# Strassen's seven products for two of the four output column blocks of a feed-forward layer

## Chip, cores and metric

The kernel runs on one core of a Trainium2 chip. The metric is the device time of one launch in microseconds, the median over several runs. The core has TensorE (PE, matrix products; its weight loads are PEld), VectorE (DVE), ScalarE (ACT), GpSimd (POOL) and SyncE (SP, which issues most DMAs). Each engine works through its own queue in order; semaphores tie the queues together.

## What is computed

A decoder trunk of two layers on a sequence of 256 tokens with 2048 features, all in float32. Layer 0 mixes by retention and pooling, layer 1 by sliding-window attention. Both end in the same kind of feed-forward block, and that block is what the change is about:

```python
def conv_glu_ffn(x, w_in, conv_w, conv_b, w_out):      # x (1, 256, 2048)
    h = x @ w_in                                       # 2048 x 11264
    hp = jnp.pad(h, ((0, 0), (2, 0), (0, 0)))
    hc = conv_b + hp[:, 0:S] * conv_w[0]
    for kk in range(1, 3):
        hc = hc + hp[:, kk:kk + S] * conv_w[kk]
    gate, val = jnp.split(hc, 2, axis=-1)
    return (jax.nn.gelu(gate, approximate=False) * val) @ w_out   # 5632 x 2048
...
x = layer_norm(ALPHA * x + ffn, ln_gain, ln_bias)
```

## The kernel before

**Weights.** All weight matrices are streamed once from HBM in groups of 128 partitions x 4 k-tiles x 512 columns (1 MB). A group s is loaded by SP into `raw[:, s % 6]` (the ring has `RING = 6` places), ScalarE rounds it to fp32r into `w_hi` (`high(s)`, L475), and VectorE writes the remainder `raw - w_hi` in place as `w_lo` (`low(s)`, L752). TensorE then makes a product of float32 quality out of three fp32r products: activations high x weights high, high x weights low, low x weights high. When it has finished a group it raises `used`; SP waits for `used` of the group six places back before it loads again. ScalarE issues `high` four groups ahead of the group that it is keeping step with (`HI_LEAD = 4`), VectorE `low` three ahead (`LO_LEAD = 3`).

**The feed-forward block.** The 5632 hidden features are cut into FC = 11 chunks of 512. For each chunk c the kernel makes

- the gate projection (`hidden`, 4 groups): the weights stand still, the 256 tokens move, once as high and low together (512 columns, L1270) and once as high alone (256 columns, L1280). The result lies in four PSUM banks, transposed;
- the value projection (`hidden`, 4 groups), into the other four banks;
- for each of two pairs of banks of either kind: ScalarE copies the low half out of PSUM (`halves`, L539), VectorE adds it (`pair_sum`, L782) and makes the causal convolution of three taps (`convolve`, L1004 and L1007); ScalarE takes the GELU of the gate, VectorE multiplies value and gate (L1027) into `gated`, and the two split that into high and low in `gT` (L622, L1032);
- the output product (`output`, 4 groups, one for each column block n of 512): for each of the two token halves of 128, twelve matmuls of 512 columns (`plain_tile`, L1297 to L1299: 4 k-tiles x 3 products). VectorE adds each block to the residual `xres` (`add_chunk`, L786, 128 x 1024).

TensorE's order is gate(0), value(0), and then nine turns of a hardware loop with gate(c+1), output(c), value(c+1) on banks 0 to 3, 4 to 7, 4 to 7; the last chunk is written out behind the loop, with output(9) and output(10) at its end, and the layer norm follows. The convolution parameters of the running chunk are copied into `cur` (L1022) since a loop can't name them.

`lnp` holds the layer norm's gain and bias (2 x 2048 words in each partition, each filled by a broadcasting load of 1 MB).

Of the kernel before, what the change touches and what calls it, by code (L numbers as in the profile page):

```python
# [52 lines left out]
ARENA = 14080  # L53
# [17 lines left out]
FFN_GROUPS = 3 * KG * FC  # L71
# [4 lines left out]
S_FFN = [S_FFN0, S_FFN1]  # L76

# [36 lines left out]
TURNS = FC - 2  # L114
LOOP_OWN = 12


class Count:


    def __init__(self):
        self.n, self.turn, self.per, self.start = 0, None, 0, 0

    def now(self):
        return self.n if self.turn is None else self.n + self.turn * self.per

    def enter(self, turn, per):
        self.turn, self.per, self.start = turn, per, self.n

    def leave(self, turns):  # L130
        assert self.n - self.start == self.per, (self.n - self.start, self.per)
        self.n, self.turn = self.start + self.per * turns, None


def build_trunk(nc, x, ln_gain, ln_bias, even_w_in, pool_w, pool_scale, even_w_out, attn_w_qkv, attn_b_qkv,
# [10 lines left out]
    with ExitStack() as ctx:  # L146
# [25 lines left out]
        ln_eps = sb("ln_eps", [P, 1])  # L172
        arena = sb("arena", [P, ARENA])

# [52 lines left out]
        conv_v = take(TPC, SEQ)  # L227
        gated = take(TPC, SEQ)
        cur = sb("cur", [P, 2, 4, TPC])
# [52 lines left out]
        ffn_added = sem("ffn_added")  # L282
        akv_ready = sem("akv_ready")
# [35 lines left out]


        @block.sync
        def _(sp):
            def load(s, source, turn=0):

                if not isinstance(turn, int) or s >= RING:

                    sp.wait_ge(used, s - RING + 1 + turn * 12)
                sp.dma_start(raw[:, s % RING], source).then_inc(raw_landed[s % RING], 16)
# [15 lines left out]
            def hidden(l, s, c, value, turn=0):  # L344
                for kg in range(KG):
                    load(s + kg, w_ffn_in[l][:, GK * kg:GK * kg + GK, bass.ds(c * COLS + value * D_FF, COLS)],
                         turn)

            def output(l, s, c, turn=0):
                for n in range(NCH):  # L350
                    load(s + n, w_ffn_out[l][:, bass.ds(c * GK, GK), cols(n * COLS)], turn)

            def ffn(l):
                base = S_FFN[l]
                hidden(l, base, 0, 0)
                hidden(l, base + KG, 0, 1)
                hidden(l, base + 2 * KG, 1, 0)
                output(l, base + 3 * KG, 0)

                sp.wait_ge(ln_chunk, TOK * NCH * (2 * l + 1))  # L360
                load_params(2 * l + 1)
                hidden(l, base + 4 * KG, 1, 1)
                with sp.Fori(1, TURNS) as turn:
                    s = base + 2 * KG
                    hidden(l, s, turn + 1, 0, turn)
                    output(l, s + KG, turn, turn)
                    hidden(l, s + 2 * KG, turn + 1, 1, turn)

                tail = base + FFN_GROUPS - 4 * KG
                hidden(l, tail, FC - 1, 0)  # L370
                hidden(l, tail + KG, FC - 1, 1)
                output(l, tail + 2 * KG, FC - 2)
                output(l, tail + 3 * KG, FC - 1)
# [74 lines left out]
        def _(pool):  # L448
# [5 lines left out]

            pool.wait_ge(gain_ready, 4)
# [10 lines left out]
        def _(act):  # L466
            def high(s, turn=0):

                if s >= S_END:
                    return  # L470
                act.wait_ge(raw_landed[s % RING], 16 * (s // RING + 1) + turn * (16 * (12 // RING)))
                if not isinstance(turn, int) or s >= RING:

                    act.wait_ge(used, s - RING + 1 + turn * 12)
                nc.scalar.activation(w_hi[:, s % RING], raw[:, s % RING], ACT.Copy).then_inc(hi_ready, 1)  # L475
# [54 lines left out]
            def halves(n, bank, ended, turn=0):  # L530

                if n == TP_ODD + 7:
                    act.wait_ge(queries_half, 1)
                else:
                    act.wait_ge(used, ended + turn * 12)
                if not isinstance(turn, int) or n >= 2:

                    act.wait_ge(added, n - 1 + turn * 4)
                nc.scalar.activation(half[:, n % 2], ps[:, bank:bank + 2, SEQ:2 * SEQ], ACT.Copy) \  # L539
                    .then_inc(half_out, 1)  # L540
# [74 lines left out]
            def gelu(n, q, turn=0):  # L615
                act.wait_ge(conv_done, n + turn * 2)
# [3 lines left out]
            def gated_high(n, q, turn=0, to=gT):  # L620
                act.wait_ge(gated_out, n + turn * 2)
                nc.scalar.activation(to[:, 2 * q:2 * q + 2, 0:SEQ], gated[:, 2 * q:2 * q + 2], ACT.Copy) \  # L622
                    .then_inc(g_hi, 1)

            def feed_forward(l):
                base, tp, gp = S_FFN[l], TP_FFN[l], 2 * FC * l
                norm_fill(2 * l, base)
                for j in range(1, 8):
# [12 lines left out]
                    if j in (6, 7):  # L641
                        gelu(gp + j - 5, j - 6)
                with act.Fori(0, TURNS) as turn:
                    s = base + 2 * KG
                    for j in range(12):
                        high(s + j + HI_LEAD, turn)
                        if j == 0:

                            for q in range(2):
# [1147 lines left out]
```

## Time and profile before

| | |
|---|---|
| median of 3 runs | 2062.64 us (2062.59 to 2062.69) |
| span of the profiled execution, first to last instruction | 2061.1 us |
| median of the runs less that span | 1.5 us |
| PE busy | 2052.3 us (100%) |
| DVE busy | 1444.6 us (70%) |
| ACT busy | 887.1 us (43%) |
| POOL busy | 5.8 us |
| read from HBM | 386.36 MB |

The profiled execution has no time of its own besides its span; the 1.5 us is what a launch has around it if the profiled execution ran like the others. An engine's busy time counts from the start of an instruction to its end; consecutive instructions of an engine can overlap by some hundredths of a microsecond, so what one costs a queue is the distance from its start to the start of the next one.

### The profile page before, as it was taken

How to read it: one execution, taken by the hardware profiler on the slowest of the kernel's cores; microseconds unless marked ns; L12 is line 12 of the kernel's file. 1: busy time of each engine (PE TensorE's matmuls, PEld its weight loads, DVE VectorE, ACT ScalarE, POOL GpSimd, SP SyncE). 2: the span in 40 equal slices, each digit the busy share in tenths (PEclk: the TensorE clock that was granted, in tenths of full speed). 3: DMA queues.
4: the chain of work that ended last, by engine and by line, in shares of the span. 5: the costliest groups of instructions: out<-in, count | busy, mean ns of one | idle time of the engine just before them, and what ended most of it. 6: DMA issues, size and time to landing. Idle time of an engine off the chain costs nothing.

```text
span 2061.1 us, 27212 instructions
## 1 busy us (share of the span) xinstructions
PE 2052.3 (100%) x10924; PEld 1756.3 (85%) x10924; DVE 1444.6 (70%) x1641; ACT 887.1 (43%) x825; POOL 5.8 (0%) x10
## 2 busy tenths in 40 slices
PE   9999999999999999999999999999999999999998
PEld 8888888888888888888888877888888888888887
DVE  5446566767767687677697886786776768766768
ACT  5433443543443434434434555354344344444342
POOL 0000000000000000000000000000000000000000
PEclk9999999999999999999999999999999999999999
DMA  9654474655555565555555435465555555555552
GB/s 331 196 191 145 142 258 163 235 197 187 188 196 186 187 198 184 186 199 184 188 186 190 144 123 190 162 241 194 194 184 193 193 184 195 191 184 195 191 184 102
DMA packets 194766, 389.57 MB, mean 189 GB/s; under 512 B 6970, under 2 KB 9748, under 8 KB 193684
## 3 DMA queue, kind: packets, MB, share of 16 engines
q1 hardware_dynamic: 194419, 388.49, 56.6%
q8 instruction: 42, 0.69, 0.1%
q10 hardware_dynamic: 288, 0.26, 0.1%
q14 instruction: 17, 0.13, 0.0%
HBM read 386.36 MB, written 2.10 MB: 188 GB/s over the span
## 4 chain that ended last, share of the span: by engine, by line
PE 98%; DVE 1%; DMA 0%; SPq 0%; issue 0%; ACT 0%; DVEq 0%
PE ps L1270 36%; PE ps L1280 19%; PE ps L1297 13%; PE ps L1299 12%; PE ps L1298 12%; PE ps L1420 1%; PE ps L1711 1%; PE ps L1686 1%; PE ps L1694 1%; PE ps L1387 0%; PE ps L1425 0%; PE ps L1258 0%; PE ps L1537 0%; DMA xres<-x 0%; DVE xres L810 0%; PE ps L1338 0%
## 5 line engine op out<-in xcount | busy, mean ns | idle before, releaser
L475 ACT ACTIVATE w_hi<-raw 128x2048 fp32r<-128x2048 f32 x352 | 673.9, 1916 | 951.1 <-DMA raw<-ffn_w_in 523.7
L752 DVE TENSOR_TENSOR w_lo<-raw,w_hi 128x2048 fp32r<-128x2048 f32 x352 | 800.9, 2287 | 220.0 <-ACT w_hi L475 219.2
L1270 PE MATMUL ps<-T,w_hi 128*128 128x512 f32 x3264 | 765.0, 390 | 0.0
L1270 PEld LDWEIGHTS ps<-T,w_hi 128*128 128x128 f32 x3264 | 605.7, 188 | 122.9 <-issue 1.7
L1280 PEld LDWEIGHTS ps<-T,w_lo 128*128 128x128 f32 x3264 | 405.8, 192 | 10.0 <-issue 2.0
L1280 PE MATMUL ps<-T,w_lo 128*128 128x256 f32 x3264 | 410.6, 283 | 0.0
L1297 PE MATMUL ps<-w_hi,gT 128*128 128x512 f32 x704 | 274.2, 389 | 0.0
L1299 PE MATMUL ps<-w_hi,gT 128*128 128x512 f32 x704 | 273.9, 389 | 0.0
L1298 PE MATMUL ps<-w_lo,gT 128*128 128x512 f32 x704 | 273.9, 389 | 0.0
L782 DVE TENSOR_TENSOR arena<-ps,half 128x512 f32<-128x512 f32 x96 | 65.5, 688 | 183.6 <-ACT half L539 183.6
L786 DVE SCALAR_TENSOR_TENSOR xres<-ps,xres 128x1024 f32<-128x1024 f32 (+1 forms) x103 | 117.9, 1144 | 89.1 <-PE ps L1299 87.9
L1297 PE MATMUL ps<-w_hi,T 128*128 128x512 f32 (+1 forms) x448 | 177.4, 396 | 0.1
L1299 PE MATMUL ps<-w_hi,T 128*128 128x512 f32 (+1 forms) x448 | 174.0, 388 | 0.0
L1298 PE MATMUL ps<-w_lo,T 128*128 128x512 f32 (+1 forms) x448 | 173.6, 388 | 0.0
L1007 DVE SCALAR_TENSOR_TENSOR arena<-arena,cur 128x256 f32<-128x256 f32 x352 | 155.1, 482 | 6.3
L1297 PEld LDWEIGHTS ps<-w_hi,gT 128*128 128x128 f32 x704 | 132.1, 188 | 28.0 <-DVE arena L1230 0.3
L1299 PEld LDWEIGHTS ps<-w_hi,gT 128*128 128x128 f32 x704 | 132.1, 188 | 27.4
L1298 PEld LDWEIGHTS ps<-w_lo,gT 128*128 128x128 f32 x704 | 132.2, 188 | 27.4
L1297 PEld LDWEIGHTS ps<-w_hi,T 128*128 128x128 f32 x448 | 84.2, 188 | 19.9 <-DVE T L843 2.7
L1299 PEld LDWEIGHTS ps<-w_hi,T 128*128 128x128 f32 x448 | 84.1, 188 | 17.6
L1298 PEld LDWEIGHTS ps<-w_lo,T 128*128 128x128 f32 x448 | 84.3, 188 | 16.2
L1004 DVE TENSOR_SCALAR arena<-arena,cur 128x256 f32<-128x256 f32 x176 | 64.7, 410 | 3.3
(159 smaller groups left out, 802.9 us busy)
## 6 DMA issues: line engine op xcount, KB each, us to landing
raw<-ffn_w_in SPq DMA_DIRECT2D x176, 1024.0 KB, 5.0
raw<-ffn_w_out SPq DMA_DIRECT2D x88, 1024.0 KB, 5.0
raw<-even_w_in SPq DMA_DIRECT2D x38, 1024.0 KB, 5.1
raw<-attn_w_qkv SPq DMA_DIRECT2D x20, 1024.0 KB, 5.2
raw<-even_w_out SPq DMA_DIRECT2D x16, 1024.0 KB, 5.0
raw<-attn_w_out SPq DMA_DIRECT2D x16, 1024.0 KB, 5.1
arena<-ln_gain SPq DMA_DIRECT2D x4, 1024.0 KB, 6.3
arena<-ln_bias SPq DMA_DIRECT2D x4, 1024.0 KB, 8.3
```

The costliest lines, as they stand in the source:

```text
L475: nc.scalar.activation(w_hi[:, s % RING], raw[:, s % RING], ACT.Copy).then_inc(hi_ready, 1)
L752: vec.tensor_tensor(w_lo[:, s % RING], raw[:, s % RING], w_hi[:, s % RING].bitcast(F32), ALU.subtract).then_inc(lo_ready, 1)
L782: vec.tensor_tensor(to, ps[:, bank:bank + 2, 0:SEQ], half[:, n % 2], ALU.add).then_inc(added, 1)
L786: return vec.scalar_tensor_tensor(at, ps[:, bank], 1.0 / ALPHA, at, ALU.mult, ALU.add)
L1004: ins = vec.tensor_scalar(conv[:, i], h[:, i, 0:SEQ], cur[:, kind, 0, i:i + 1], cur[:, kind, 3, i:i + 1], ALU.mult, ALU.add)
L1007: ins = vec.scalar_tensor_tensor(conv[:, i], h[:, i, k:k + SEQ], cur[:, kind, k, i:i + 1], conv[:, i], ALU.mult, ALU.add)
L1270: ins = mm(ps[:, banks[j]], w_hi[:, s % RING, k, P * j:P * j + P], T[:, GK * kg + k], start=kg == 0 and k == 0, stop=kg == KG - 1 and k == ...
L1280: ins = mm(ps[:, banks[j], 0:SEQ], w_lo[:, s % RING, k, P * j:P * j + P], T[:, GK * kg + k, 0:SEQ], start=False, stop=False)
L1297: mm(ps[:, bank, 0:n], x_hi, w_hi[:, s % RING, k, c], start=start and k == 0, stop=False)
L1298: mm(ps[:, bank, 0:n], x_hi, w_lo[:, s % RING, k, c], start=False, stop=False)
L1299: ins = mm(ps[:, bank, 0:n], x_lo, w_hi[:, s % RING, k, c], start=False, stop=stop and k == GK - 1)
L1420: mm(ps[:, a], T[:, t, lo:lo + P], w_hi[:, s, k], start=False, stop=False)
```

## The change

Two chunks of hidden features, a = 2p and b = 2p + 1, are taken together (a "duo", five in each layer, `DUOS = 5`; chunk 10 is left over and goes through an ordinary output product, the tail). For column blocks 0 and 1 the product [256 tokens x 1024 hidden] x [1024 x 1024 columns] is cut into 2 x 2 blocks: token halves x the two chunks on one side, the two chunks x the two column blocks on the other. Seven products of blocks replace eight. Each needs a form of the activations (a block of `gated` or a difference of such: `X_11, X_21, D_3, X_12, X_22, D_1, D_2, D_4`) and a block or sum of blocks of the weights (`SUM_12, W_11, W_22, SUM_24, SUM_124, W_21, SUM_ALL`). Column blocks 2 and 3 keep the plain product, with the two chunks summed in PSUM before they are read (`pair_output`).

- Weights of the seven (names as indices 0 to 6 in TensorE's order): `W_11`, `W_22`, `W_21` are loaded. `SUM_24` is loaded with one block, and GpSimd then issues two DMAs, one behind the other, of two k-tiles each (512 KB), that add the fourth block from HBM onto it. `SUM_12`, `SUM_124` and `SUM_ALL` are additions on VectorE (128 x 2048 each). The first two stand in `weight_sums`, the third in `last_weight_sum`. They are put in the place of `lnp`, which is loaded only near the end of the layer.
- Order on TensorE in a duo: gate(a+2), value(a+2), the seven products (`quad`), gate(b+2), value(b+2), four groups of `pair_output`.
- The seven results go from PSUM to `xres` in nine additions of 128 x 512 (`take_product`), some with the sign -1; three of them read a bank into which two or three products were summed.
- Each group that is only a sum takes a place in `w_hi` but none in the ring of loads.
- The hardware loops are gone: the program is written out, and `cur` with it.

The core of the diff:

```diff
+            for l in range(2):                       # GpSimd
+                for p in range(DUOS):
+                    i, q = DUOS * l + p, S_FFN[l] + Q_AT[p]
+                    pool.wait_ge(*landed(q + SUM_24))
+                    pool.wait_ge(summed, 3 * i + 1)
+                    for j in range(2):
+                        t = GK * (2 * p + 1) + 2 * j
+                        pool.dma_start(raw_at(q + SUM_24)[:, 2 * j:2 * j + 2], w_ffn_out[l][:, t:t + 2, COLS:2 * COLS],
+                                       accum_op=ALU.add).then_inc(second_summed, 16)
+                        pool.wait_ge(second_summed, 32 * i + 16 * (j + 1))
...
+                if s in SUMS and SUMS[s][0] == SUM_24:          # ScalarE, high(s)
+                    act.wait_ge(second_summed, 32 * (DMA_SUMS.index(s) + 1))
+                elif s in SUMS:
+                    act.wait_ge(summed, SUMS[s][1])
+                else:
+                    act.wait_ge(*landed(s))
...
+                def weight_sums(p):                             # VectorE
+                    q, n = base + Q_AT[p], 3 * (DUOS * l + p)
+                    dve.wait_ge(*landed(q + W_11))
+                    dve.wait_ge(*landed(q + SUM_24))
+                    vec.tensor_tensor(raw_at(q + SUM_12), raw_at(q + W_11), raw_at(q + SUM_24), ALU.add) \
+                        .then_inc(summed, 1)
+                    dve.wait_ge(*landed(q + W_22))
+                    dve.wait_ge(summed, n + 1)
+                    vec.tensor_tensor(raw_at(q + SUM_124), raw_at(q + SUM_12), raw_at(q + W_22), ALU.add) \
+                        .then_inc(summed, 1)
...
+                    s = base + V_AT[a]
+                    for j in range(KG):
+                        if j < 2:
+                            gate_pair(a, j, x)
+                        if j == 1:
+                            weight_sums(p)
+                        low(s + j + LO_LEAD)
+                    s = base + Q_AT[p]
+                    low(s + LO_LEAD)
+                    dve.wait_ge(used, s + 1)
+                    last_weight_sum(p)
+                    take_product(p, 0, x, 1, 1, -1.0)
+                    low(s + 1 + LO_LEAD)
+                    dve.wait_ge(used, s + 2)
+                    take_product(p, 1, x + 1, 0, 0, 1.0)
+                    low(s + 2 + LO_LEAD)
+                    dve.wait_ge(used, s + 3)
+                    take_product(p, 2, x, 0, 1, -1.0)
+                    low(s + 3 + LO_LEAD)
+                    dve.wait_ge(used, s + 4)
+                    take_product(p, 3, x + 3, 1, 1, -1.0, 1)
+                    low(s + 4 + LO_LEAD)
+                    dve.wait_ge(used, s + 5)
+                    take_product(p, 4, x + 1, 0, 1, -1.0, 3)
+                    take_product(p, 5, x + 1, 1, 0, 1.0)
+                    take_product(p, 6, x + 1, 1, 1, -1.0, 4)
+                    dve.wait_ge(used, s + 6)
+                    take_product(p, 7, x + 2, 0, 0, 1.0, 2)
+                    dve.wait_ge(used, s + 7)
+                    take_product(p, 8, x + 3, 1, 0, 1.0, 6)
...
+                s = base + C_AT[DUOS - 1]                       # VectorE, end of a layer
+                for j in range(KG):
+                    if j == 2:
+                        dve.wait_ge(used, s + 2)
+                        add_chunk(2, 0, ffn_added)
+                    low(s + j + LO_LEAD)
+                    if j < 2:
+                        value_pair(c, j, 4)
+                    else:
+                        gated_low(j - 2)
...
+            def form_product(s, f, bank, start, stop=True, more=False):     # TensorE
+                for k in range(GK):
+                    x_hi, x_lo = form_at(f)[:, k, 0], form_at(f)[:, k, 1]
+                    w, last = w_hi[:, s % RING, k], stop and k == GK - 1
+                    mm(ps[:, bank], x_hi, w, start=start and k == 0, stop=False, skip_group_check=more)
+                    mm(ps[:, bank], x_hi, lo_at(s)[:, k], start=False, stop=False, skip_group_check=more)
+                    ins = mm(ps[:, bank], x_lo, w, start=False, stop=last, skip_group_check=more)
+                return ins
...
+                def quad(p, x):
+                    s, r = base + Q_AT[p], READS * (DUOS * l + p)
+                    pe.wait_ge(form_ready, FORMS * (DUOS * l + p + 1))
+                    pe.wait_ge(*evicted(2 * p + 2, 0)[1])
+                    ready(s)
+                    form_product(s + SUM_12, D_1, x, True).then_inc(used, 1)
+                    ready(s + W_11)
+                    form_product(s + W_11, X_11, x + 1, True).then_inc(used, 1)
+                    ready(s + W_22)
+                    pe.wait_ge(quad_read, r + 1)
+                    form_product(s + W_22, D_4, x, False, more=True).then_inc(used, 1)
+                    ready(s + SUM_24)
+                    form_product(s + SUM_24, D_3, x + 3, True).then_inc(used, 1)
...
+                    out_block(l, q + W_11, a, 0)                # SP, order of loads in a duo
+                    out_block(l, q + W_22, b, 1)
+                    out_block(l, q + SUM_24, a, 1)
+                    out_block(l, q + W_21, b, 0)
```

`quad_read` counts the nine `take_product` of a duo; the third product waits for the first of them, the fifth for the second, the seventh for the fourth, and gate(b+2) for the seventh and the ninth. SP's load of a group waits for `used` of the load six places back in the ring of loads, which for `SUM_24` is the first group of value(a+2), and for `W_21` the second.

## Rows read from the trace of the kernel before

**Rows 1.** The page: busy time by engine, clock in 40 slices, the chain.
```profile
PE 2052.3 (100%) x10924; PEld 1756.3 (85%) x10924; DVE 1444.6 (70%) x1641; ACT 887.1 (43%) x825; POOL 5.8 (0%) x10
...
PEclk9999999999999999999999999999999999999999
...
PE 98%; DVE 1%; DMA 0%; SPq 0%; issue 0%; ACT 0%; DVEq 0%
```

**Rows 2.** Timeline of PE: start us, us, engine, line, names, shapes, count.
```profile
564.18 3.79 PE L1270 MATMUL ps<-T,w_hi 128*128 128x512 f32 x16
567.81 4.00 PE L1280 MATMUL ps<-T,w_lo 128*128 128x256 f32 x32
571.64 7.44 PE L1270 MATMUL ps<-T,w_hi 128*128 128x512 f32 x32
...
608.64 0.39 PE L1297 MATMUL ps<-w_hi,gT 128*128 128x512 f32 x1
608.86 0.39 PE L1298 MATMUL ps<-w_lo,gT 128*128 128x512 f32 x1
...
630.40 3.79 PE L1270 MATMUL ps<-T,w_hi 128*128 128x512 f32 x16
```

**Rows 3.** Groups of DVE over two turns of the loop, 602 to 734.2.
```profile
L752 DVE TENSOR_TENSOR w_lo<-raw,w_hi 128x2048 fp32r<-128x2048 f32 x25 | 57.0, 2287 | 16.4 <-ACT w_hi L475 16.2
L1007 DVE SCALAR_TENSOR_TENSOR arena<-arena,cur 128x256 f32<-128x256 f32 x32 | 14.1, 482 | 0.6
L786 DVE SCALAR_TENSOR_TENSOR xres<-ps,xres 128x1024 f32<-128x1024 f32 x8 | 9.8, 1223 | 6.0 <-PE ps L1299 5.9
```

**Rows 4.** Busy times in stretches: engines, clock, DMA share, GB/s.
```profile
602.00:734.20 132.20, 132.20 (x705) 114.54 (x704) 93.62 (x101) 54.12 (x40) 0.00 (x0) 1.00 0.58 190
10.00:15.00 5.00, 4.59 (x28) 4.11 (x29) 3.82 (x7) 3.17 (x6) 0.00 (x0) 1.00 1.05 401
2055.00:2061.00 6.00, 0.67 (x2) 0.00 (x0) 3.35 (x5) 0.69 (x1) 0.00 (x0) 0.93 0.66 253
```

**Rows 5.** Timeline of DVE in one turn of the loop.
```profile
588.72 0.69 DVE L782 TENSOR_TENSOR arena<-ps,half 128x512 f32<-128x512 f32 x1 [3.75 <-ACT half L539]
...
592.76 2.28 DVE L752 TENSOR_TENSOR w_lo<-raw,w_hi 128x2048 fp32r<-128x2048 f32 x1
594.97 0.68 DVE L782 TENSOR_TENSOR arena<-ps,half 128x512 f32<-128x512 f32 x1
...
601.19 0.69 DVE L1032 TENSOR_TENSOR gT<-arena,gT 128x512 fp32r<-128x512 f32 x1
601.79 2.28 DVE L752 TENSOR_TENSOR w_lo<-raw,w_hi 128x2048 fp32r<-128x2048 f32 x1
...
614.28 1.23 DVE L786 SCALAR_TENSOR_TENSOR xres<-ps,xres 128x1024 f32<-128x1024 f32 x1
615.42 2.28 DVE L752 TENSOR_TENSOR w_lo<-raw,w_hi 128x2048 fp32r<-128x2048 f32 x1
```

**Rows 6.** Timeline of ACT: the wait for a load, and a split after it.
```profile
575.16 1.92 ACT L475 ACTIVATE w_hi<-raw 128x2048 fp32r<-128x2048 f32 x1 [3.48 <-DMA raw<-ffn_w_in]
580.65 1.91 ACT L475 ACTIVATE w_hi<-raw 128x2048 fp32r<-128x2048 f32 x1 [3.57 <-DMA raw<-ffn_w_in]
```

**Rows 7.** DMA issues: count, KB each, median us from issue to landing.
```profile
raw<-ffn_w_out SPq DMA_DIRECT2D x88, 1024.0 KB, 5.0
...
xres<-x SPq DMA_DIRECT2D x3, 512.0 KB, 7.7
...
out<-xres SPq DMA_DIRECT2D x2, 512.0 KB, 3.1
out<-xres SPq DMA_DIRECT2D x4, 256.0 KB, 2.5
```

**Rows 8.** The residual's addition for one token half, over the whole span.
```profile
L786 DVE SCALAR_TENSOR_TENSOR xres<-ps,xres 128x512 f32<-128x512 f32 x15 | 10.3, 685 | 11.4 <-PE ps L1299 11.3
```

More of the change, by code:

```diff
@@ L113 @@
 BURSTS = PAIRS + 3
-TURNS = FC - 2
-LOOP_OWN = 12
 class Count:
     def __init__(self):
[L122 to L132, printed above, removed]
+        self.n = 0
 def build_trunk(nc, x, ln_gain, ln_bias, even_w_in, pool_w, pool_scale, even_w_out, attn_w_qkv, attn_b_qkv,
@@ L342, in even_in, with hidden @@
                 load(s, w_even_in[:, GK * kg:GK * kg + GK, cols(EVEN_COLS[c])])
-            def hidden(l, s, c, value, turn=0):
+            def hidden(l, s, c, value):
                 for kg in range(KG):
[L346 to L351, printed above, removed]
+                    load(s + kg, w_ffn_in[l][:, GK * kg:GK * kg + GK, cols(c * COLS + value * D_FF)])
@@ L353, in ffn, with out_block @@
+            def out_block(l, s, c, n):
+                load(s, w_ffn_out[l][:, GK * c:GK * c + GK, cols(n * COLS)])
             def ffn(l):
                 base = S_FFN[l]
[L355 to L373, printed above, removed]
+                def chunk(c):
+                    hidden(l, base + G_AT[c], c, 0)
+                    hidden(l, base + V_AT[c], c, 1)
@@ new lines, in feed_forward @@
+                tail, c = base + TAIL_AT, FC - 1
+                s = base + C_AT[DUOS - 1]
+                for j in range(KG):
+                    if j == 2:
+                        dve.wait_ge(used, s + 2)
+                        add_chunk(2, 0, ffn_added)
+                    low(s + j + LO_LEAD)
+                    if j < 2:
+                        value_pair(c, j, 4)
+                    else:
+                        gated_low(j - 2)
+                dve.wait_ge(used, tail)
+                add_chunk(3, 2, ffn_added)
@@ L1605, in turn_gate, with hidden @@
                     ins.then_inc(gate_turned, 1)
-                def hidden(s, bank, turn=0, waits=(), gate=False):
+                def hidden(at, bank, waits=(), gate=False):
+                    s = base + at
                     for kg in range(KG):
@@ new lines, in pair_output @@
+                def pair_output(p, x, waits):
+                    for i in range(KG):
+                        s, bank = base + C_AT[p] + i, x + 2 * (i // 2)
+                        ready(s)
+                        if i % 2 == 0:
+                            pe.wait_ge(*waits[i // 2])
+                        for a, f in enumerate(((X_11, X_21), (X_12, X_22))[i % 2]):
+                            ins = form_product(s, f, bank + a, i % 2 == 0, i % 2 == 1)
+                        ins.then_inc(used, 1)
```

531 lines of the change are left out of this document (352 added, 179 removed).

## Prediction

> **What bounds the kernel now.** I read the page's busy times first, then its chain of waits. TensorE is busy 2052.3 of 2061.1 us, and 98% of the chain that ends last is its matmuls, with no slice of the clock line below nine tenths [rows 1]. So a matmul that is taken out is worth its time, as long as nothing else becomes late. Who could? Over two turns of the loop (two chunks, what is now a duo), VectorE is busy 93.62 of 132.2 us, ScalarE 54.12, and the DMA engines work 0.58 of the time at 190 GB/s [rows 4]. VectorE is the nearest to its limit, but its busy share is an average. The question is what it must do while the seven products run, since each of them lasts half as long as a group does today.
>
> **What TensorE loses.** Today's 4 groups of an output product are 96 matmuls from 608.64 to 630.40, 0.2267 us each; a hidden group takes (608.64 - 564.18)/8 = 5.56 us, an output group 5.44 [rows 2]. In column blocks 0 and 1 a duo has 2 chunks x 2 blocks x 2 token halves x 12 = 96 matmuls now, and 7 x 12 = 84 afterwards. Blocks 2 and 3 keep their 96. That is 12 x 0.2267 = 2.72 us for each duo, and **27.2 us** for ten. A product of the seven takes 2.72 us and is one whole group for `high` and `low`.
>
> **What VectorE gains in work.** What an instruction costs its queue is the distance to the next start: `low` 594.97 - 592.76 = 2.21; a split of 128 x 512 601.79 - 601.19 = 0.60; `add_chunk` 1.14; a pair's sum, convolution and product 592.76 - 588.72 = 4.04 [rows 5]. I take `take_product` at 0.61 in the queue, 0.69 to its end, by the 685 ns of the same operation on 128 x 512 [rows 8], and a weight sum as a `low`: two SBUF operands, same shape, 2.21 in the queue and 2.29 to its end [rows 3]. A duo gets 3 more `low` and 3 sums (+13.3), 4 more form splits and 4 differences (+4.9), and nine reads and two `add_chunk` instead of eight (9 x 0.61 + 2 x 1.14 - 8 x 1.14 = -1.4). So some 17 us are added to 93.6, in 129.5: 85%. On average it fits. ScalarE (3 more `high` of 1.9, 4 more forms) stays near 50%.
>
> **The walk through the seven products**, in us after the first matmul of value(a+2), for any duo. TensorE's ideal times: seven products from 4 x 5.56 = 22.2 on, one each 2.72; the third at 27.7; the next group at 41.3.
> The load of `SUM_24`'s first block waits for the first value group. From the end of such a group to the `high` of the load it frees is now 575.16 - (564.18 + 5.56) = 5.4 [rows 2, 6], so it is there at 5.56 + 5.4 = 11.0. VectorE has by then done both gate pairs and a `low` (0.8 + 3.4 + 2.2 + 3.4 = 9.8) and waits for it. `SUM_12` runs 11.0 to 13.3, `SUM_124` to 15.6, then `low` of products 0, 1, 2 to 22.2. TensorE starts in time.
> At 13.3 GpSimd may issue its first adding DMA. Call A the time from an issue to its landing: the second has landed at 13.3 + 2A. ScalarE's split, waiting there with every later `high` behind it, ends 1.95 later, and `low` of product 3 begins at 15.3 + 2A. Behind it in VectorE's queue stand the last weight sum, which must also wait until product 0 is done (24.9 + 0.2), and the read of product 0, for which product 2 waits because it sums into that bank. If A is short, the sum starts at 25.1, the read ends at 25.1 + 2.2 + 0.7 = 28.0 plus hops, 28.1: product 2 starts 0.4 late. If A is long, it starts at 15.3 + 2A + 2.2 + 2.9 = 20.4 + 2A, so **2A - 7.2 us late; the two cases meet at A = 3.8**. After it VectorE needs 2.21 + 0.61 = 2.8 for a product and TensorE 2.72, but VectorE is one step ahead: the seventh product needs three further `low` and reads (8.6 against 10.9 us of products 2 to 5), the next gate group a fourth `low` and three reads (12.7 against 13.6). So the stall occurs once in a duo, and isn't caught up, since TensorE has no slack to give back.
>
> **The price of A.** The trace of before has no adding DMA and none from GpSimd. Nearest rows: 1 MB from HBM lands in 5.0 us, 512 KB stores in 3.1, 256 KB stores in 2.5 [rows 7]. In the crowded start the engines move 401 GB/s [rows 4], 2.6 us for 1 MB; of the 5.0, 2.4 are then fixed and 2.6 moving. A plain 512 KB load would take 2.4 + 1.3 = 3.7, my lower end. The addition must also read the 512 KB that lie in SBUF: by bytes read it is the 1 MB row, **A = 5.0**, which I take. Upper end: the weight stream keeps 0.58 of the engines busy meanwhile, so 2.6 us of moving become 2.6/0.42 = 6.2, A = 8.6 (the crowded 512 KB loads at the start took 7.7). Of weight loads only one and a half fall into those 10 us, hence nearer to 5.0 than to 8.6.
> The Trainium skill, in Collectives: The Full Stack, Part 3 (Why 7x under link rate), says that the addition in a DMA costs no cycles, but that its second source read halves the rate (1.93 measured there). As an estimate from that page, 1.3 x 1.93 + 2.4 makes A = 4.9 and a sum 2 us lower; no run here shows it.
> With A = 5.0 each duo loses 2.8 us, **28 us** for ten.
>
> **The end of a layer.** Chunk 10's value is worked on while the last four groups of `pair_output` run (4 x 5.44 = 21.8). VectorE's queue from their start: the ninth read (0.8), three `low` (6.6), value pair (4.0), `low` (2.2), value pair (4.0), `add_chunk` (1.1), `low` (2.2), split (0.6), `low` (2.2), split (0.7): 24.5. The tail product needs the last split: **2.8 us late, 5.6 in two layers**. Bounds: nothing if the queue is ahead by then, 8 if it comes in later by a stage. Today output(9) starts with less in front of it and no wait shows in the chain [rows 1].
> Free, and why: the loads (the same bytes at a share of 0.58 as before [rows 4], since only the engine that issues the fourth block's load changes); `load_params` late in the layer, behind two tail loads and ahead of two, whose groups are needed 20 us later; the first duo, whose forms (8 x 0.61), two value pairs and four `low` make 21.8 against 22.2 in a stage; the written-out program: the two mixers are already straight code, and issue is 0% of the chain [rows 1]. If one of these covers goes, the price is some us each, in the range.
>
> **The sum**, on the profiled execution: 2061.1 - 27.2 + 28 + 5.6 = 2067.5 of span, and with the 1.5 us that separate the median of the runs from that span, **2069 us**. In general 2041 + 10 max(0.4, 2A - 7.2): break-even at A = 4.7.
>
> **Rivals.** *The adding DMA is no dearer than a plain one* (faster). The read from SBUF runs beside the read from HBM, A is at most 3.8 by the lower end, the stall is 0.4: 2041 + 4 = 2045. For it: DMA engines are free 0.42 of the time. Against it: descriptors made by GpSimd, two completions in sequence. It decides for faster up to A = 4.5. The Trainium skill, in DMA: Bandwidth & Descriptors (Anatomy of one DMA), gives a GpSimd-issued DMA 2.0 us and its bytes at 436 GB/s, an estimate of 3.2 us for 512 KB, and by that the sum is 2045; it says nothing there of an addition.
> *The weight stream crowds it* (A = 8.6): 10 us lost in each duo, 2141.
> *The clock falls in the gaps.* In the one stretch where TensorE is nearly idle, 2055 to 2061, the granted clock is 0.93 [rows 4]. If each gap put the remaining five products (13.6 us) at the lower of its two levels (1.2 instead of 2.4 GHz), each duo would cost up to 13.6 more: 2205. Against it: gaps of 3 us are far shorter than that idle end.
> *The products give nothing*, as VectorE ends the stage anyway: the walk leaves it 0.9 us before gate(b+2). If a `take_product` or a sum were 10% dearer that margin goes: some 1 us a duo, 10 in all. It is inside the range.
>
> **Chances and range.** Forecast, A from 4.9 to 6.2 (2067 to 2093): 0.42. Faster rival, A below 4.5: 0.36. Between them, A from 4.5 to 4.9, no change that can be told (0.2%, 4.1 us, is about what a measurement of this kernel can tell): 0.12. Crowded or clocked down: 0.10. So faster 0.36, same 0.12, slower 0.52. The range takes in the faster rival and leaves out the last: 2043 to 2100.
>
> **What the changed trace would show.** Ten gaps before the third product's matmuls, with VectorE as releaser and behind it ScalarE waiting for the DMA that GpSimd issued: 2.8 us each if I am right, 0.4 in the first rival. From issue to landing 5.0 us for 512 KB in the DMA view. 120 matmuls fewer (two layers). A gap of 2.8 before each tail. Clock 1.00 throughout. I am wrong if these DMAs take under 4.5 or over 6.2, or if the gaps stand elsewhere: before the first product (forms or `weight_sums` late) or in gate(b+2).

## The result: 3.6% slower

The changed kernel takes 2138.98 us (median of 4 runs, 2132.03 to 2140.80), the kernel before 2062.61. The ratio is 1.0364, with a 95% interval of 1.035 to 1.0378. That is 76 us more, 70 above the forecast of 2069 and beyond its range, on the side that had the larger chance. All comparisons are of undisturbed runs: one launch of the kernel before, among those beside the experiments on the place of the forms, took 7495 us and is left out.

The page of the changed kernel, busy times, the slices of PE, the chain, and the DMA issues that matter; to be held against [rows 1] and [rows 7]:

```profile
span 2138.5 us, 25599 instructions
PE 2059.1 (96%) x10804; PEld 1749.2 (82%) x10804; DVE 1601.8 (75%) x1767; ACT 961.0 (45%) x895; POOL 30.3 (1%) x30
...
PE   9999999998989989899899999999898998989988
...
PE 82%; DMA 9%; DVE 6%; issue 2%; ACT 1%; SPq 0%; POOLq 0%; DVEq 0%
...
raw<-ffn_w_out SPq DMA_DIRECT2D x88, 1024.0 KB, 5.1
...
raw<-ffn_w_out POOLq DMA_DIRECT2D x20, 512.0 KB, 6.1
```

The 120 matmuls are gone (10924 to 10804). But PE is busy 6.8 us more than before where it should be 27 less, its slices in the two feed-forward blocks have holes, and the chain goes through a DMA for 9% of the span. The DMAs that GpSimd issued take 6.1 us each, against 5.1 for twice the bytes issued by SyncE.

What PE waited for (engine, line, released by: us in total, times, longest):

```profile
PE ps L1865 <- DVE xres L1257: 67.0, 10, 10.2
PE ps L1563 <- DVE T L1195: 4.0, 2, 2.0
```

These are ten waits, one in each duo, for `take_product` (L1257), and one at the end of each layer. The chain through the second duo shows what stands behind such a wait (start, us, what):

```profile
597.88 5.33 DMA raw<-ffn_w_out
603.30 2.30 DVE arena L1237
605.67 0.56 issue
606.23 6.06 DMA raw<-ffn_w_out
612.29 0.44 issue
612.73 6.00 DMA raw<-ffn_w_out
618.75 1.92 ACT w_hi L566
620.76 2.15 issue
622.90 2.29 DVE arena L1249
625.19 0.61 DVE xres L1257
625.93 0.76 PE ps L1865
626.70 0.43 PE ps L1866
627.12 0.43 PE ps L1867
```

Read it downwards: the load of `SUM_24`'s block, the first weight sum (L1237), GpSimd's first adding DMA, its second, ScalarE's split, VectorE's split of product 3 (it stands here as "issue"; VectorE's timeline has it from 620.69, 2.29 long), the last weight sum, the read of product 0, and only then product 2. From the end of the first sum to the landing of the second DMA it is 618.73 - 605.60 = 13.1 us. The matmuls after the wait are 0.43 us apart. Before it they were 0.23. The same stretch, and that of the duo after it, in the windows (PE busy, PEld, DVE, ACT, POOL, clock, DMA share, GB/s):

```profile
625.93:630.93 5.00, 5.00 (x12) 3.94 (x13) 4.86 (x3) 3.00 (x2) 0.00 (x0) 0.51 0.00 0
765.10:770.10 5.00, 5.00 (x12) 3.95 (x13) 4.85 (x3) 2.99 (x2) 0.00 (x0) 0.50 0.01 3
```

After each of the ten idle gaps, 5.4 us or longer, the granted clock was half, that is 1.2 instead of 2.4 GHz, for 2.9 to 5.7 us of matmuls, 46 us over all ten.

### The profile page after: what moved, and what is told of

Its sections match the earlier page's. It is cut to its first block, busy times and chain, and to the rows that moved or that the text cites. A ratio compares the mean times of both kernels' runs of the same rounds, so it can differ in the third digit from the quotient of the medians.

```text
span 2138.5 us, 25599 instructions
## 1 busy us (share of the span) xinstructions
PE 2059.1 (96%) x10804; PEld 1749.2 (82%) x10804; DVE 1601.8 (75%) x1767; ACT 961.0 (45%) x895; POOL 30.3 (1%) x30
## 4 chain that ended last, share of the span: by engine, by line
PE 82%; DMA 9%; DVE 6%; issue 2%; ACT 1%; SPq 0%; POOLq 0%; DVEq 0%
PE ps L1536 30%; PE ps L1546 16%; DMA raw<-ffn_w_out 9%; PE ps L1865 5%; PE ps L1563 5%; PE ps L1866 5%; PE ps L1867 5%; PE ps L1565 5%; PE ps L1564 5%; DVE w_lo L913 1%; DVE arena L1237 1%; DVE arena L1249 1%; ACT w_hi L566 1%; PE ps L1686 1%; PE ps L2015 1%
## 5 line engine op out<-in xcount | busy, mean ns | idle before, releaser
L1865 PE MATMUL ps<-w_hi,forms 128*128 128x512 f32 x400 | 168.4, 421 | 67.0 <-DVE xres L1257 67.0
L1867 PE MATMUL ps<-w_hi,forms 128*128 128x512 f32 x400 | 165.9, 415 | 0.0
L1174 DVE SCALAR_TENSOR_TENSOR arena<-arena,taps 128x256 f32<-128x256 f32 x352 | 155.1, 482 | 6.3
L1865 PEld LDWEIGHTS ps<-w_hi,forms 128*128 128x128 f32 x400 | 80.7, 202 | 90.0 <-issue 70.9
L630 ACT ACTIVATE half<-ps 128x512 f32<-128x512 f32 x104 | 56.3, 593 | 159.2 <-PE ps L1536 151.9
L1866 PE MATMUL ps<-w_lo,forms 128*128 128x512 f32 x280 | 118.8, 424 | 0.0
L566 ACT ACTIVATE w_hi<-arena 128x2048 fp32r<-128x2048 f32 x30 | 57.2, 1908 | 129.8 <-DVE arena L1237 120.2
L1867 PEld LDWEIGHTS ps<-w_hi,forms 128*128 128x128 f32 x400 | 80.2, 200 | 20.0
L947 DVE SCALAR_TENSOR_TENSOR xres<-ps,xres 128x1024 f32<-128x1024 f32 (+1 forms) x43 | 44.5, 1035 | 66.2 <-PE ps L1565 37.4
```

Of the source, the lines that this page charges most:

```text
L566: nc.scalar.activation(w_hi[:, s % RING], raw_at(s), ACT.Copy).then_inc(hi_ready, 1)
L1174: ins = vec.scalar_tensor_tensor(conv[:, i], h[:, i, k:k + SEQ], tap(k), conv[:, i], ALU.mult, ALU.add)
L1865: mm(ps[:, bank], x_hi, w, start=start and k == 0, stop=False, skip_group_check=more)
L1866: mm(ps[:, bank], x_hi, lo_at(s)[:, k], start=False, stop=False, skip_group_check=more)
L1867: ins = mm(ps[:, bank], x_lo, w, start=False, stop=last, skip_group_check=more)
```

## The experiments

Every duo is the same, so one number per duo is worth ten in the time. "Gap" is PE's wait before a product. Theory: **the two adding DMAs in sequence are longer than I took them for; product 2 pays for them because its read stands behind the waiting split; the gap then costs a second time through the clock.** Rivals: VectorE is full in this stage whatever the DMAs do; the DMAs are slow because of GpSimd's issue, not because of the addition; the slow matmuls have a cause of their own.

**Without the adding DMAs**

```diff
-                pool.dma_start(raw_at(q + SUM_24)[...], w_ffn_out[l][...], accum_op=ALU.add)...
-                if s in SUMS and SUMS[s][0] == SUM_24:
-                    act.wait_ge(second_summed, 32 * (DMA_SUMS.index(s) + 1))
-                elif s in SUMS:
+                if s in SUMS and s not in LOAD_OF:
```

> The GpSimd DMAs are left out: the fourth product of a duo uses one weight block where the reference needs the sum of two, and ScalarE's split of it waits for the SyncE load alone. Theory (the two adding DMAs in sequence make the gap, and the gap makes the clock fall): the third product is 0.4 us late at most, the granted clock is 1.00 in the products, and the time is 2062.6 - 27.2 (matmuls) + 4 (ten gaps of 0.4) + 4 (tail, as in the changed kernel's trace) + 8 (matmuls on the forms at 0.233 instead of 0.227 us) = 2051 us. Rival (VectorE's queue is too full in the products whatever the DMA does): gaps of several us stay, 2090 us or more.

Measured: 2055.90 us, ratio 0.9969 (0.9956 to 0.9981). The waits:

```profile
PE ps L1550 <- DVE T L1182: 4.0, 2, 2.0
PE ps L1852 <- DVE xres L1244: 3.1, 10, 0.3
```

The gaps shrink from 6.7 to 0.3 us and the clock of the run is 1.000. From the changed kernel's span to this one it is 2138.5 - 2054.1 = 84.4 us: 67.0 - 3.1 = 63.9 of gaps, and 20.5 more. That remainder fits the clock: the 46 us at half of it, with matmuls 0.43 us apart instead of 0.234, lose 21. VectorE's fullness as the cause of the large gaps is out. The time is 5 above the 2051 that I expected. What is left against the sum of the terms (2061.1 - 27.2 + 3.1 + 4.0 = 2041.0 of span) is 13 us, where I expected 8 for slow matmuls on the forms: in the second duo the seven products take 20.1 us, where the old distance gives 19.0 and the wait of 0.3, and `pair_output` takes 22.1 against 21.8.

**One adding DMA of 1 MB for two of 512 KB**

```diff
-                    for j in range(2):
-                        pool.dma_start(raw_at(q + SUM_24)[:, 2 * j:2 * j + 2], ..., accum_op=ALU.add)...
-                        pool.wait_ge(second_summed, 32 * i + 16 * (j + 1))
+                    pool.dma_start(raw_at(q + SUM_24), w_ffn_out[l][:, t:t + GK, COLS:2 * COLS],
+                                   accum_op=ALU.add).then_inc(second_summed, 16)
...
-    dynamic_dma_scratch_size=1024
+    dynamic_dma_scratch_size=2048
```

The larger DMA comes with a larger scratch; what the scratch alone does was not tried.

> One adding DMA of 1 MB in each duo in place of two of 512 KB in sequence (descriptor scratch 2048 instead of 1024 bytes). Theory that most of the 6.1 us of a 512 KB DMA is fixed (issue, receipt), moving 1.3: issue to landing about 7.5 to 8, the sum of the pair's 13.1 becomes 8 to 8.5, the gap 1 to 1.5 us, no fall of the clock worth naming: 2060 to 2067 us. Rival that the addition halves the rate and so most of the 6.1 is moving: 10 to 11 us to landing, gap 3 to 4 us, 2085 to 2110.

**The same two DMAs, copying instead of adding**

```diff
-                        pool.dma_start(..., w_ffn_out[l][:, t:t + 2, COLS:2 * COLS], accum_op=ALU.add)...
+                        pool.dma_start(..., w_ffn_out[l][:, t:t + 2, COLS:2 * COLS])...
```

> The same two GpSimd DMAs copy instead of adding, so the fourth block replaces the third in the sum; everything else, waits too, as in the changed kernel. If the addition (a second read, from SBUF) is what is dear: landing falls from 6.1 to about 3.7 to 4.5 us, the gap from 6.7 to 1.5 to 3, the time to about 2065 to 2085. If it is GpSimd's issue and the receipts in sequence: landing stays at 5.5 to 6.1 and the time within 15 us of the changed kernel's 2139.

Measured: 2089.81 us (1.0133, 1.0116 to 1.015) and 2093.32 us (1.0143, 1.0126 to 1.016). The DMA issues of the first, then of the second:

```profile
raw<-ffn_w_out POOLq DMA_DIRECT2D x10, 1024.0 KB, 9.2
```
```profile
raw<-ffn_w_out POOLq DMA_DIRECT2D x20, 512.0 KB, 4.6
```

These are three prices: adding 512 KB 6.1, adding 1 MB 9.2, copying 512 KB 4.6. By the two adding sizes, 3.1 us are moving for 512 KB and 3.0 are fixed. With the same fixed part a copy moves 512 KB in 1.6, so by this split the addition nearly doubles the moving part (1.9; that the copy has the same fixed part is assumed). The Trainium skill's rule in Collectives: The Full Stack, Part 3, a second source read halves the rate, 1.93 there, agrees with that. The pages of the changed kernel and of the one with copies have a second measure, how long GpSimd's queue held the DMA engines (packets, MB, share of the span):

```profile
q0 software_dynamic: 5440, 10.49, 3.2%
```
```profile
q0 software_dynamic: 2880, 10.49, 1.4%
```

The same bytes hold the engines 2.3 times as long when they are added. Neither of my two bets for the single DMA held: it landed between them, at 9.2, and so did the gap, 2.6, while the time lies in the range of the second, 2085 to 2110. Of the copies I expected 3.7 to 4.5 us, a gap of 1.5 to 3 and at most 2085: the addition is most of what was too dear, but the time is 8 above, since the clock fell behind four of the eight gaps of 2.4 to 3.0 us and behind the two longer ones.
PE's waits were 25.7 us in ten gaps with one DMA and 29.8 with the copies. By the walk's formula, with 0.6 us from the sum to GpSimd's issue and 0.4 to 0.5 between the two copies, the DMAs' stretch is 9.8 and some 10.3, and the gap 2.6 and 3.1 us. Measured, as means, were 2.6 and 3.0. With the changed kernel's 13.1 it gives 5.9, and eight of its ten gaps were 5.4 to 7.2.

**The gap filled with matmuls**

```diff
+                    for _ in range(22):
+                        mm(ps[:, x + 2, 0:P], ident[:], ident[:], start=True, stop=True)
                     ready(s + W_22)
```

> 22 matmuls of the 128 x 128 identity on itself into a free bank are put between the second and the third product, about 5.2 us of work in the gap; their result isn't used. Theory that the idle gap lowers the granted clock to half for some 5 us after it: the clock stays at 1.00, the third product's matmuls are 0.23 us apart instead of 0.43, and ten times 2.3 us come back: 2116 us. Rival that the slow matmuls after the gap have another cause (their operands): no gain, 2139, or more by the dummies.

Measured: 2122.69 us (1.0279, 1.0259 to 1.0299). The DMAs took as long as before (6.2). In seven of the ten duos the filling left a wait of 0.7 to 1.2 us, in three 2.8 to 5.2. A duo of either kind, the first matmul after the wait on PE's timeline (the number in brackets is the wait), and the window behind it:

```profile
1646.71 0.47 PE L1865 MATMUL ps<-w_hi,forms 128*128 128x512 f32 x1 [0.74 <-DVE xres L1257]
...
631.69 0.77 PE L1865 MATMUL ps<-w_hi,forms 128*128 128x512 f32 x1 [4.76 <-DVE xres L1257]
```
```profile
631.69:636.69 5.00, 5.00 (x12) 3.94 (x13) 4.86 (x3) 3.00 (x2) 0.00 (x0) 0.50 0.00 0
1646.71:1651.71 5.00, 5.00 (x22) 4.04 (x23) 5.00 (x4) 4.88 (x3) 0.00 (x0) 1.00 0.12 23
```

Twelve matmuls in 5 us after the idle gap, 22 after the filled one, product and operands the same: the slow matmuls are the clock's, and idleness brings the clock down. By the medians 16 us came back of the 20.5. I had expected 23, for all ten gaps.

**The reads ahead of the waiting split**

```diff
-                    low(s + LO_LEAD)
                     dve.wait_ge(used, s + 1)
                     last_weight_sum(p)
                     take_product(p, 0, x, 1, 1, -1.0)
-                    low(s + 1 + LO_LEAD)
                     dve.wait_ge(used, s + 2)
                     take_product(p, 1, x + 1, 0, 0, 1.0)
+                    low(s + LO_LEAD)
+                    low(s + 1 + LO_LEAD)
```

> VectorE's order in the products is changed: the last weight sum and the reads of products 0 and 1 stand before the split of product 3 (the one that waits for the adding DMAs), the DMAs themselves are untouched. Theory (the gap is the DMAs' 13.1 us, but product 2 pays it only because its read stands behind the waiting split): product 2 is 0.4 us late at most; product 3 needs its split at 15.3 + 13.1 + 2.2 = 30.6 us of the stage against its own start at 30.8, so it waits next to nothing where the DMAs take their usual time, and 3 to 4 us in the one duo of each layer whose DMAs took 17 us. About 2056 (as without the DMAs) + 2 x 5 = 2060 to 2068 us. Rival (VectorE can't catch up after a late split of product 3): the gap moves to products 4 to 6 or to the next gate group and stays at 3 us or more in each duo, 2095 or more.

Measured: 2073.10 us (2067.53 to 2075.34; 1.0049, 1.0033 to 1.0065). 66 us come back with the DMAs untouched (6.1 us each). The waits:

```profile
PE ps L1563 <- DVE T L1195: 4.1, 2, 2.1
PE ps L1865 <- DVE w_lo L913: 3.9, 1, 3.9
PE ps L1865 <- DVE xres L1257: 3.5, 11, 0.4
PE ps L1536 <- DVE xres L1257: 3.0, 8, 0.4
```

One long gap is left in the profiled run, in the last duo, for a late split of product 3 itself; elsewhere 0.3 us before product 2 and 0.4 before the next gate group. So it was the place in VectorE's queue that made TensorE pay for the DMAs; with only product 3's split behind them, 13.1 us fit nine times out of ten. The median lies 5 us above what I expected at most: the runs differ by 8, where the kernel before differs by under 1, and the one gap shows DMAs that come some us late now and then. The changed kernel has two such pairs, in the fourth duo of layer 0 and the last of layer 1, with gaps of 9.9 and 10.2. The chain through the first of them:

```profile
884.39 7.82 DMA raw<-ffn_w_out
892.21 0.36 issue
892.57 8.72 DMA raw<-ffn_w_out
```

The packets in the trace show the order. In the eight usual pairs the second DMA is issued 6.2 to 6.6 us after the first and its packets start 1.9 us later. SyncE's next weight load is issued 7.7 to 8.7 us after the first, and its packets come behind them, in two duos partly between them. In the two late pairs the first DMA takes 7.8 and 8.0 us, the second is issued after 8.2 and 8.4, the load's packets get in front of it, and its own start 5.0 to 5.2 us after its issue. The late pair of this run is like them (second issue after 7.9, packets 4.2 later). What holds up the first is less sure: in both, a 16 KB packet of an instruction queue (0.9 us) starts 5.8 to 6.0 us after the issue, where a usual first DMA has its last packets, and in the usual pairs none does. But in this experiment's fourth duo such a packet did no harm, and no run removes it.

**32 bytes of pad**

```diff
+        sb("pad", [P, 8])
         with nc.sbuf_tensor("sum_lo", [P, 2, GK, COLS], F32R) as sum_lo:
```

> A pad of 32 bytes in each partition ahead of the arena moves the forms from byte address 197088 (32 beyond a multiple of 64) to 197120 (a multiple of 128). Nothing else changes. Theory that the matmuls whose stationary operand is one of the six forms in the arena are 0.233 us apart instead of 0.227 because of this misalignment (those on the two forms in gT, at a multiple of 128, are not slow): they come to 0.227, 1200 matmuls of 0.006, 8 us less: 2131. Rival (the difference has another cause, such as the way high and low alternate in the forms): no change beyond 2 us.

Measured: 2135.01 us (1.035, 1.0334 to 1.0366). 4 us below the changed kernel's median, within the spread of its runs; the theory had 2131. It fails on the matmul starts too: in the second duo's `pair_output` 24 matmuls on the forms in the arena take 5.59 us with the pad, 5.61 in the changed kernel, and 5.44 on gT's forms.

**Reads first, the pad, and the tail's order**, with this edit besides the two above:

```diff
                     else:
                         gated_low(j - 2)
+                    low(s + j + LO_LEAD)
...
-                    low(s + j + LO_LEAD)
                     if j < 2:
                         value_pair(c, j, 4)
```

> Reads first as in e5_reads_first, the pad of e6_aligned, and at the end of a layer each value pair and gated split ahead of the weight split of its step. If all three theories hold: 2055.9 (without the adding DMAs) - 8 (pad) - 4 (two tail gaps) + 5 to 10 (late DMAs in two duos) = 2049 to 2054 us, faster than the kernel before by 0.4 to 0.6%. If the pad does nothing: 2057 to 2062.

Measured: 2067.38 us (2062.59 to 2073.20 in 9 runs; 1.0027, 1.0017 to 1.0037). The waits at the tails are gone, worth 4 to 6 us, which was what this edit was for. The pad brings nothing that can be seen. The forecast for the case that all three theories hold was 13 us too low, that for a pad without effect (2057 to 2062) 5: the late DMAs cost more than I allowed, with one gap of 3.8 in the profiled run and a spread of 11 us between runs.

**A plain load, and the addition on VectorE**, on top of the three edits before:

```diff
+                    sp.dma_start(lnp[:, 0]..., w_ffn_out[l][:, GK * b:GK * b + GK, cols(COLS)]).then_inc(second_summed, 16)
                     out_block(l, q + W_11, a, 0)
...
+                    vec.tensor_tensor(raw_at(q + SUM_24), raw_at(q + SUM_24), lnp[:, 0]..., ALU.add) \
+                        .then_inc(block_added, 1)
...
                     dve.wait_ge(used, s + 1)
                     last_weight_sum(p)
                     take_product(p, 0, x, 1, 1, -1.0)
                     low(s + LO_LEAD)
                     dve.wait_ge(used, s + 2)
                     take_product(p, 1, x + 1, 0, 0, 1.0)
                     low(s + 1 + LO_LEAD)
```

> As e8_combined, but the fourth block is a plain SyncE load into the place of the layer norm's gain, long before it is needed, and VectorE adds it (one more 128 x 2048 addition a duo, 2.2 us); GpSimd issues nothing. VectorE's queue by the walk: products 0, 1, 2 split by 19.9, 22.1, 24.3, last sum 27.3, first read 28.0, split of product 3 30.2, read 1 30.8, split of product 4 33.0: nothing is over 0.5 us late. 2055.9 - 8 - 4 = 2044 us, up to 2050 if the queue loses some tenths more in each duo; no duo has a long gap. Rival (VectorE is full in this stage, so 2.2 us more is 2.2 us of gap): 2065 to 2075.

Measured: 2056.37 us (2056.26 to 2058.29 in 8 runs; 0.9971, 0.9961 to 0.9982): 0.3% faster than the kernel before. Without GpSimd's DMAs the runs differ by 2 us and not by 11. The waits:

```profile
PE ps L1873 <- DVE xres L1264: 4.4, 12, 0.4
PE ps L1544 <- DVE xres L1264: 3.4, 8, 0.4
```

No gap in the duos is over 0.43 us. The short waits make 7.8 us, as in the kernel with the adding DMAs and the same reads first (7.6), so 2.2 us more on VectorE in each duo can't be seen. Of the 12 us above my 2044, 8 are what the pad was to bring, and nearly 5 are these waits, which were 3.1 in the kernel without the DMAs. The slow matmuls are still there. Their starts in the `pair_output` of the second duo: 24 on gT's forms take 5.44 us (0.2267 each), the next 24 on the arena's forms 5.59 (0.2329), then 5.46 and 5.59.

**The forms at another place**

```diff
-        xres = sb("xres", [P, TOK, D])
+        (sum_lo, front, forms, arena: first of all)
         T = sb("T", [P, KT, 2 * SEQ], F32R)
...
         gT = sb("gT", [P, TPC, 2 * SEQ], F32R)
+        xres = sb("xres", [P, TOK, D])
```

The second version also puts `gT` below the weight rings.

> As e9_vector_sum, but the arena is allocated first, so the six forms move from byte 197120 of each partition to 36032; gT moves to 191680 to 199871, xres above it. Theory (a stationary operand that lies high in a partition, beyond 192 KB = 196608, makes a matmul of 512 columns take 0.234 instead of 0.227 us): the matmuls on the forms come to 0.227 (120 a duo, 0.9 us), and those on the form X_21, which now lies at 195776 to 199871, become slow (24 a duo, 0.2 us): 2056.4 - 9 + 2 = 2049 us. Rival (the slow matmuls have to do with what the forms are, not where): the forms stay at 0.234, no change from 2056.

> As e10_forms_low, with gT ahead of the weight rings, so that all forms lie below 196608 and only the last 3264 bytes of the raw ring's last place reach beyond it. Theory of the place: all form matmuls at 0.227, 2056.4 - 9 = 2047 us, 0.7% faster than the kernel before. Rival: 2056.

Measured: 2053.72 us (0.996, 0.9946 to 0.9974) and 2053.48 us (0.9958, 0.9944 to 0.9972). The form matmuls by line, of the kernel with the vector sum and then of the first of these (count, busy, mean ns, idle before):

```profile
L1873 PE MATMUL ps<-w_hi,forms 128*128 128x512 f32 x400 | 158.7, 397 | 3.5 <-DVE xres L1264 3.5
...
L1875 PE MATMUL ps<-w_hi,forms 128*128 128x512 f32 x400 | 157.8, 394 | 0.0
```
```profile
L1872 PE MATMUL ps<-w_hi,forms 128*128 128x512 f32 x400 | 156.8, 392 | 3.2 <-DVE xres L1263 3.2
...
L1874 PE MATMUL ps<-w_hi,forms 128*128 128x512 f32 x400 | 155.9, 390 | 0.0
...
L1874 PE MATMUL ps<-w_hi,gT 128*128 128x512 f32 x200 | 78.0, 390 | 0.0
```

All four runs of 24 in `pair_output` now take 5.44. So the slow matmuls come from where the forms lie, not from what they are. That it is their own place, and not their distance from another buffer, isn't shown for certain, since the other buffers moved too; two different orders of the rest gave the same time. The boundary that I supposed at 196608 is not the cause: most of X_21 lay beyond it in the first of the two, and the matmuls on gT stayed at 390 ns. I expected 7 and 9 us, and 3 came off. PE's busy time fell by 4.8 (2038.4 to 2033.6), and 2 of them went into waits for VectorE, the one before the next gate group above all: from 3.4 to 5.0 us in eight duos.

**One read ahead of the last weight sum**

```diff
-                    last_weight_sum(p)
                     take_product(p, 0, x, 1, 1, -1.0)
+                    last_weight_sum(p)
```

> As e11_all_low, with the read of product 0 ahead of the last weight sum. The wait of 0.3 to 0.4 us before product 2 goes (the read is done 0.9 us after product 0 instead of 3.1). VectorE has the same work, and it is busy from there to the next gate group, so by the theory that its queue ends the stage, the wait before that group grows by what the first one loses and the time stays at 2053 us; if the two waits are independent, ten times 0.35 = 3.5 us come off, 2050.

Measured: 2053.65 us (0.9956, 0.9942 to 0.997). The waits:

```profile
PE ps L1543 <- DVE xres L1263: 8.0, 8, 1.0
PE ps L1872 <- DVE xres L1263: 2.0, 2, 1.0
```

The wait before product 2 is gone, and the one before the next group is 1.0 us instead of 0.6, in all ten duos: the time stays, as the first of the two theories had it. VectorE's work in the stage sets its end. Of the 27.2 us that the matmuls give, 9 arrive. Of the other 18, these waits are 10. Nearly 8 are PE's own busy time, 2033.0 against 2052.3 - 27.2 = 2025.1, and most of them lie in the seven products, which in the kernel before this one take 20.6 us in a duo where 19.0 and 0.9 of waits were to be expected. Why is open.

## Why the prediction was wrong

**TensorE's loss of matmuls** held: 120 fewer, 2.72 us a duo.

**The walk** held to tenths. It put the first weight sum at 11.0 us of the stage. In the second duo the first product starts at 614.38, the four value groups therefore 22.2 before it, at 592.1, and the sum came at 603.3, 11.2 later. Its formula, 2A - 7.2, gives 5.9 with the measured stretch of 13.1, and 2.6 and 3.1 for the two variants. That VectorE isn't the cause of the large gaps, and that product 2, not product 3, pays, are shown by leaving out the DMAs and by the reordering.

**The larger failure is a size, the price of A.** I took the 1 MB row, 5.0, by the bytes read. It is 6.1 from issue to landing, inside the 6.2 that I had named as the sign of being wrong. But the walk put the two DMAs end to end, and there are 0.6 us from the sum to the issue and 0.4 between the two: 13.1 for the pair, 6.55 each. The fixed part was as I had it. In the usual pairs the first packet starts 1.9 us after the issue and the landing is 0.3 us after the last, 2.2 against my 2.4. The moving part was not: mostly 3.8 us for 512 KB against my 2.6. (The split by the two sizes above puts it lower and the fixed part higher; the packets are the direct measure.) I had doubled the bytes and kept the rate of a plain load. Two stretches of the changed kernel, the end of a weight load and the middle of the adding DMA behind it, show what doubling the bytes leaves out (PE busy, PEld, DVE, ACT, POOL, clock, DMA share, GB/s):

```profile
744.90:746.90 2.00, 2.00 (x15) 1.80 (x14) 2.00 (x2) 2.00 (x2) 1.20 (x1) 1.00 1.02 389
747.00:750.00 3.00, 3.00 (x26) 2.96 (x26) 3.00 (x2) 3.00 (x3) 0.00 (x0) 1.00 1.00 154
```

The engines are full in both, at 389 GB/s for the load and 154 for the addition. With the bytes read out of SBUF counted on top that is 308, still less than 389. The weight stream was a small part of it: in the usual pairs its packets, at the two ends of an addition, mostly took 5 to 15% of the engines' time. Only in the two late pairs did a load get in front, and there the second DMA took the 8.7 and 8.9 us of the rival with the crowded stream. With 6.55 in place of 5.0 the gaps are 59 us and not 28; the two late pairs bring them to 67. That is 39 of the missing 70: some 21 the DMAs themselves, 10 the hops, 8 the late pairs.

**The step that failed as a mechanism is the clock, which the sum had at nothing.** I priced it as a rival and set it aside, since gaps of 3 us were far shorter than the idle end. In the runs all gaps of 3.5 us or more brought it down, and shorter ones, from 2.0 us on, sometimes did: even with the forecast gap of 2.8 it would have been a term, not nothing. From the kernel with one DMA, the waits of the first and the second duo, and the windows behind them:

```profile
484.72 0.47 PE L1863 MATMUL ps<-w_hi,forms 128*128 128x512 f32 x1 [2.37 <-DVE xres L1255]
...
618.08 0.47 PE L1863 MATMUL ps<-w_hi,forms 128*128 128x512 f32 x1 [2.39 <-DVE xres L1255]
```
```profile
618.08:623.08 5.00, 5.00 (x15) 3.99 (x16) 5.00 (x4) 3.59 (x3) 0.00 (x0) 0.66 0.43 166
484.72:489.72 5.00, 5.00 (x22) 4.04 (x23) 5.00 (x4) 4.86 (x3) 0.00 (x0) 1.00 0.58 186
```

The waits are the same within 0.02 us, and once the clock fell and once not. It cost 20.5 us in the changed kernel, not the 136 of the rival: the clock is back before 6 us of matmuls are over, not after all five products.

**A term was missing**: TensorE's own time for the products, 13 us in all (2054.1 - (2061.1 - 27.2) - 3.1 - 4.0 = 13.1 in the kernel without the DMAs). I had priced them by the matmuls of today, whose operands lie elsewhere. Some 5 of the 13 went when the forms were moved; the other 8 are in every version, and their cause is open.

**The tail** was right in kind: 2.0 us late in each layer against 2.8.

Together: 2069 + 39 (gaps) + 20.5 (clock) + 13 (the products' own time) - 1.6 (tail) = 2140, measured 2139. That the crowded rival's 2141 is nearly the measured time is chance: it had gaps of 10 us in each duo, and they were 6.7. The forecast's direction, slower, was right for its reason, but the loss was to be 6 us and is 76. I cut the range at 2100 by leaving out the crowded and clocked-down cases together, at 0.10, although a longer A makes longer gaps and so brings the clock down too: they are not two rivals, they add up.

**The version that wins** keeps Strassen's products, drops the adding DMA, has the reads first and the forms in another place: 2053.5 us against 2062.4, 0.4% faster than the kernel before and 85 us below the changed one.

## What to carry to other kernels

A step on the critical queue that waits for a slow thing must not stand ahead of work that is ready: moving two reads and a sum past the waiting split gave back 66 us without touching the DMAs. An idle gap on TensorE has two prices, its length and the slower matmuls behind it, so a forecast with gaps of several us should add the second as a term and not as a rival. And when the product count falls, look at which engine serves each product: here the shorter products hand the end of the stage to VectorE, which takes 10 of the 27 us, and a third of the saving is what arrives.

## What the runs showed of the hardware

- An adding DMA issued by GpSimd onto SBUF: 6.1 us for 512 KB and 9.2 for 1 MB from issue to landing, beside the weight stream; a copy of 512 KB by the same engine 4.6; SyncE's plain load of 1 MB 5.1. Of the 6.1, 1.9 pass before the first packet and 0.3 after the last. While it adds, the engines are full at 154 GB/s, and at 389 under a plain load. GpSimd's issue instruction itself is 1.2 us for the addition and 0.72 for the copy.
- Two of ten such DMA pairs came 4 to 5 us late: a first DMA that took 7.8 to 8.0 us let the next weight load in front of the second. Kernels with adding or copying DMAs of GpSimd's spread over 3 to 13 us from run to run, those without over 0.3 to 2.1.
- The granted clock after an idle gap: half for up to 6 us after gaps of 3.5 to 10.4 us; after 2.0 to 3.0 us sometimes lowered and sometimes 1.00; after gaps of up to 1.2 us lowered in none of the products of these runs.
- Moving the stationary operands, and other buffers with them, from 197088 bytes on in each partition down to 36032 changed the distance of 512-column matmuls from 0.233 to 0.2267 us. It is neither the 32 bytes' misalignment nor a boundary at 196608 bytes; what it is stays open.
